# Unrolling the first layer of a two-layer encoder step, with score jobs in pairs and the weights' low parts on VectorE

## What is computed

```
for i in range(2):                                     # layer 0: diff, layer 1: fox
    h = rmsnorm(x, norm_mix[i])
    x = x + mixer(h) @ w_o                             # 1024x1024
    h = rmsnorm(x, norm_ffn[i])
    gate, up = split(h @ w_in, 2)                      # 1024 x 2*2816
    x = x + (silu(gate) * up) @ w_out                  # 2816x1024
y = rmsnorm(x, norm_final)

def diff_mixer(h):                                     # per group: two heads share V
    q, k, v = split(h @ w_qkv); q, k = rope(q), rope(k)
    p1, p2 = softmax(q1 @ k1.T / 8 + mask), softmax(q2 @ k2.T / 8 + mask)
    o = (p1 - lam * p2) @ v
    return rmsnorm(o, subln) * 0.8
```

## Time and profile before

| | us |
|---|---|
| median of 3 runs (lowest to highest) | 1607.44 (1604.28 to 1611.6) |
| the profiled execution | 1607.57 |
| its span, first to last instruction | 1605.4 |
| TensorE busy in the span | 1563.1 |
| VectorE / GpSimd / ScalarE busy | 619.9 / 581.5 / 560.9 |

### The profile page before, as it was taken

One profiled execution on the slowest core, in us unless ns is written; L12 is line 12 of the kernel. 1 busy time (PEld: TensorE's weight loads), 2 busy tenths in 40 slices (PEclk: granted clock), 3 DMA queues, 4 the chain that ended last, 5 costly groups with the idle time before them and its releaser, 6 DMA issues.

```text
span 1605.4 us, 29879 instructions
## 1 busy us (share of the span) xinstructions
PE 1563.1 (97%) x11071; PEld 1476.8 (92%) x11071; DVE 619.9 (39%) x1091; ACT 560.9 (35%) x995; POOL 581.5 (36%) x276
## 2 busy tenths in 40 slices
PE   6999999999999999999999999999999999999996
PEld 5888888999999999999978888888999999999996
DVE  6667776451111111121366666665521111111212
ACT  4455545442222222222334444444332222232221
POOL 3333233334544444333322222221344455444331
PEclk9999999999999999999999999999999999999998
DMA  5322223122222222222211211111122222222222
GB/s 188 98 85 83 95 85 107 41 79 79 78 82 88 78 78 85 76 82 85 94 62 61 62 60 60 60 57 48 67 79 85 85 78 78 91 78 74 83 83 82
DMA packets 44628, 128.49 MB, mean 80 GB/s; under 512 B 5648, under 2 KB 10256, under 8 KB 44576
## 3 DMA queue, kind: packets, MB, share of 16 engines
q1 hardware_dynamic: 44576, 127.79, 23.6%
HBM read 111.21 MB, written 11.83 MB: 77 GB/s over the span
## 4 chain that ended last, share of the span: by engine, by line
PE 91%; DVE 5%; issue 2%; ACT 1%; DMA 1%; SPq 0%; DVEq 0%; ACTq 0%
PE ps L486 73%; PE sps L534 3%; PE ops L597 3%; PE tps L554 2%; PE sps L540 2%; PE sps L535 2%; PE sps L536 2%; PE sps L542 1%; PE ops L587 1%; DVE acc L1164 1%; DVE aug_l L1303 1%; DVE xT L1173 0%; PE tps L568 0%; DVE ptl L1269 0%; PE ops L604 0%
## 5 line engine op out<-in xcount | busy, mean ns | idle before, releaser
L1069 POOL TENSOR_TENSOR w_lo<-w_raw,w_hi 128x1024 fp32r<-128x1024 f32 (+1 forms) x199 | 469.4, 2359 | 922.2 <-ACT w_hi L787 922.2
L486 PE MATMUL ps<-xh,w_hi 128*128 128x288 f32 x2176 | 489.5, 307 | 18.5 <-DVE xl L1418 11.5
L486 PE MATMUL ps<-xl,w_hi 128*128 128x288 f32 x2176 | 468.7, 297 | 0.0
L486 PE MATMUL ps<-xh,w_lo 128*128 128x288 f32 x2176 | 468.3, 297 | 0.0
L486 PEld LDWEIGHTS ps<-xh,w_hi 128*128 128x128 f32 x2176 | 350.2, 191 | 20.4 <-issue 19.9
L787 ACT ACTIVATE w_hi<-w_raw 128x1024 fp32r<-128x1024 f32 (+1 forms) x200 | 208.3, 1042 | 451.7 <-PE ps L486 449.5
L486 PEld LDWEIGHTS ps<-xh,w_lo 128*128 128x128 f32 x2176 | 352.9, 190 | 0.0
L486 PEld LDWEIGHTS ps<-xl,w_hi 128*128 128x128 f32 x2176 | 352.8, 190 | 0.0
L866 ACT ACTIVATE pr<-sps,nmax 128x384 f32<-128x384 f32 (+3 forms) x160 | 85.9, 537 | 205.4 <-DVE nmax L1233 188.4
L486 PE MATMUL ps<-hh,w_hi 128*128 128x288 f32 x704 | 150.9, 295 | 0.0
L486 PE MATMUL ps<-hl,w_hi 128*128 128x288 f32 x704 | 150.8, 295 | 0.0
(11 more groups left out here) (154 smaller groups left out, 1768.6 us busy)
## 6 DMA issues: line engine op xcount, KB each, us to landing
w_raw<-w_units SPq DMA_DIRECT2D x184, 512.0 KB, 3.2
w_raw<-w_units SPq DMA_DIRECT2D x16, 384.0 KB, 2.8
qsw<-qsin SPq DMA_DIRECT2D x64, 72.0 KB, 2.0
xT<-x_in SPq DMA_DIRECT2D x8, 288.0 KB, 5.6
dk_out<-kf SPq DMA_DIRECT2D x8, 288.0 KB, 2.1
dv_out<-vf SPq DMA_DIRECT2D x8, 288.0 KB, 4.1
fk_out<-kf SPq DMA_DIRECT2D x8, 288.0 KB, 4.1
fv_out<-vf SPq DMA_DIRECT2D x8, 288.0 KB, 4.0
```

Source lines behind the costliest of these rows:

```text
L486: mm = nc.tensor.matmul(out[:, half, :], w[:, k, :], rhs[:, kt, half * HALF:(half + 1) * HALF], start=start and w is w_hi[slot] and rhs is ...
L1069: nc.gpsimd.tensor_tensor(w_lo[slot][:, 0:kts, :], w_raw[slot][:, 0:kts, :], w_hi[slot][:, 0:kts, :].bitcast(F32), ALU.subtract).then_inc( ...
```

## The change

The first layer is written out whole, without loops, by a count t of slots from its start. Each engine goes through all t and has, for every step of a group's attention, a slot of its own in tables (`D_SCORE`, `D_MAX`, `D_EXP`, ...; s is the slot counted from the start of the next group). Beside that:

- `score_pair` takes the place of two score jobs.
- the first head's scaling goes from VectorE to ScalarE (`weigh_first`), and each head has a reciprocal of its own.
- VectorE makes w_lo of units 2 to 24 (`weight_lo`); GpSimd keeps the others.
- in both layers V is split straight out of PSUM, in three pieces, vl by VectorE (`v_lo`); the cached V has a buffer v_raw.
- the head norm's squares are made by ScalarE; GpSimd has nothing left in the first layer's groups.
- in both layers the output projection has 14 runs in another order, and the preparation of the tiles is spread over its steps by tables (`WO_RES_AT`, `WO_HI_AT`, `WO_LO_AT`, `WO_SQ_AT`, `WO_SUM_AT`), with two buffers for the squares. The norm sum moves from slice 6 of the FFN's first unit to slice 2 of its second, and in the second layer's first unit from slice 6 to its end.
- SP issues the first layer's transfers by the same count t.

```diff
+WO_STEPS = ([(j, 4 + j, k) for j in (0, 1, 2) for k in range(6)]
+            + [(j, j - 2, k) for j in (3, 4, 5) for k in range(7)]
+            + [(6, 0, k) for k in range(KT)]
+            + [(6 + t, t, 7) for t in (1, 2, 3)]
+            + [(6 + t, t, k) for t in (4, 5, 6) for k in (6, 7)]
+            + [(13, 7, k) for k in range(KT)])
...
+D_SCORE, D_MAX, D_EXP, D_DEN, D_SCALE, D_MIX = (3, 5, 11, 14, 19), (2, 5, 10, 13, 20), ...
+D_TURN, D_TAKE_P, D_P_LO = (8, 12, 17, 19, 27), (8, 12, 16, 21, 26), (7, 12, 15, 19, 26)
+D_W_LO = 3
+D_SPLIT = 1
...
+            def score_pair(a, par, p):
+
+                i = JOBS[DIFF][2 * p][0]
+                if some(a * 10 + 2 * p):
+                    pe.wait_ge(exp_done, val(a * 10 + 2 * p))
...
+                for x, y, first in ((qh, kh, True), (qh, kl, False), (ql, kh, False)):
+                    for h in range(2):
+                        b = slice(64 * h, 64 * h + 64)
+                        nc.tensor.matmul(sps[:, h, 0:width(i)], x[par][b, q], y[par][b, k], start=first, stop=False)
+                d = 0 if i == 4 else i
+                for h in range(2):
+                    nc.tensor.matmul(sps[:, h, P * d:P * d + P], ident16, mask[DIFF], start=False, stop=True
+                                     ).then_inc(s_done, 1)
...
-                        if tt == 0:
-                            pe.wait_ge(vr_done, val((a + (G * L + 1)) * 2))
+                            pe.wait_ge(vl_done, val((a + G) * 3 + 1))
...
-                    if k == 6 and norm > 0:
-                        norm_sum(norm)
...
                 if L == FOX:
-
+                    norm_sum(2)
                     pe.wait_ge(f_hi_done, 1)
                     pe.wait_ge(f_lo_done, 1)
                     pe.wait_ge(r_ready, 3)
...
+                    if k == NORM_AT:
+                        norm_sum(2 * L + 1)
...
+            def weigh_first(a, par, p):
+
+                w, tau, sa = width(JOBS[DIFF][2 * p][0]), a.c * 5 + p, (10 * par + 2 * p) % 4
+                act.wait_ge(rden_done, 2 * tau + 1)
+                nc.scalar.activation(pr[:, sa, 0:w], pr[:, sa, 0:w], ACT.Copy, scale=rden[:, sa:sa + 1]
+                                     ).then_inc(pa_done, 1)
...
+            def weight_lo(u):
+
+                slot = u % 2
+                dve.wait_ge(w_hi_done, u + 1)
+                dve.wait_ge(w_used, u - 1)
+                tt(w_lo[slot][:], w_raw[slot][:], w_hi[slot][:].bitcast(F32), ALU.subtract).then_inc(w_lo_done, 1)
...
+            def v_lo(L, a):
+
+                gi = a + G * L
+                for b, hi, src in ((0, vh[:, 0:4, :], tps[:]), (1, vh[:, 4, :], ops[:, 0:P]), (2, vh[:, 5:7, :], v_raw[:])):
+                    dve.wait_ge(vh_done, val(gi * 3 + (b + 1)))
+                    dst = (vl[:, 0:4, :], vl[:, 4, :], vl[:, 5:7, :])[b]
+                    tt(dst, src, hi.bitcast(F32), ALU.subtract).then_inc(vl_done, 1)
...
+                    if t % KT == D_W_LO and KT <= t < SLOTS * G:
+                        weight_lo(t // KT + 1)
+                    if t >= SLOTS * G:
+                        wo_residuals(DIFF, t - SLOTS * G)
+                    diff_attention(t)
```

More of the change, by code:

```diff
@@ L220, in encoder @@
         hf = place("hf", [P, T])
-        sqt = place("sqt", [P, T], offset=ARENA - 4 * T)
+        sqt = [place(f"sqt{s}", [P, T], offset=ARENA - 4 * T * (s + 1)) for s in range(2)]
         sq_all = place("sq_all", [P, KT, T], offset=o_at)
@@ L619, in attention @@
-                for tt in range(len(T_AT[L])):
-                    if T_AT[L][tt] == slot:
+                    if S_AT[FOX][jj] == slot:
+                        score(a, par, jj)
+                for tt in range(len(T_AT[FOX])):
+                    if T_AT[FOX][tt] == slot:
                         if tt == 0:
-                            pe.wait_ge(vr_done, val((a + (G * L + 1)) * 2))
-                            if L == DIFF and not first:
-                                pe.wait_ge(oln_done, val(a))
-                        transpose_p(L, a, par, tt)
@@ L636, in group, with project @@
+            def project(L, g, slot):
+                u, n = g * 3 + U_LAYER * L, g * 3 + N_LAYER * L
+                part, k = slot // KT, slot % KT
+                if k == 0:
+                    open_unit(u + part, n + part)
+                mm = slice_(u + part, n + part, k, xh, xl, k, k == 0, k == KT - 1)
+                if k == KT - 1:
+                    mm.then_inc(w_used, 1)
+            def group(g, par, first=False):
                 lag = 1 if first else 0
@@ L728, in _ @@
+                mm = slice_(Num(u + q // KT), Num(n + j), q % KT, oh, ol, k, q == WO_OPEN[j], q == WO_END[j])
+                if q % KT == KT - 1:
+                    mm.then_inc(w_used, 1)
+                elif q == WO_END[j]:
+                    mm.then_inc(wo_done, 1)
             for L in (DIFF, FOX):
                 first_group(L)
-                group(L, Num(1), 1, first=True)
-                with pe.Fori(0, 3) as it:
-                    for par in range(2):
-                        group(L, Num(2 + par, 2, it), par)
@@ L924, in attention, with wo_prep, fox_attention @@
+            def wo_prep(L, q):
+                for k in range(KT):
+                    if WO_HI_AT[k] == q:
+                        act.wait_ge(ps_read, N_LAYER * L + N_WO + 6 + k + 1)
+                        prep_hi(2 * L + 1, Num(k))
+                    if WO_SQ_AT[k] == q:
+                        prep_square(2 * L + 1, Num(k))
+            def fox_attention(a, par, slot, first=False):
                 if slot == 0 and not first:
-                    take_o(L, a - 1, L)
+                    take_o(FOX, a - 1, 1)
@@ L945, in attention, with group @@
+                for h in range(2):
+                    if PVS_AT[FOX][h] == slot:
+                        take_o_sample(FOX, a, h)
+                    if PVP_AT[FOX][h] == slot:
+                        take_o(FOX, a, h)
+                    if PVS_AT[FOX][h] + 1 == slot:
                         o_hi_sample(a, h)
-            def group(L, g, par, first=False, alone=False):
-                u = g * 3 + U_LAYER * L
+            def group(g, par, first=False, alone=False):
+                u = g * 3 + U_LAYER
@@ L949, in group @@
                 for slot in range(SLOTS):
                     if not alone:
-                        attention(L, g - 1, 1 - par, slot, first)
-                    if alone and L == FOX and slot == 0:
+                        fox_attention(g - 1, 1 - par, slot, first)
+                    if alone and slot == 0:
                         act.wait_ge(f_loaded, 16)
@@ L1320, in attention @@
[L1320 to L1326 removed]
+                    if S_AT[FOX][jj] + 1 == slot:
+                        weigh(a, par, jj)
+                for t in range(len(T_AT[FOX])):
+                    if T_AT[FOX][t] == slot:
+                        p_lo(FOX, a, t)
@@ L1327, in attention, with group @@
+                for h in range(2):
+                    if PVS_AT[FOX][h] == slot:
+                        o_sum(FOX, a, h)
+                    if PVS_AT[FOX][h] + 2 == slot:
                         o_lo_sample(a, h)
-                    if PVP_AT[L][h] == slot:
+                    if PVP_AT[FOX][h] == slot:
                         o_lo(a, h)
-            def group(L, g, par, first=False, alone=False):
+            def group(g, par, first=False, alone=False):
                 for slot in range(SLOTS):
```

702 lines of the change are left out of this document (390 added, 312 removed).

## The result

The changed kernel takes 1569.91 us (median of 4 runs, 1567.91 to 1570.72), the kernel before 1608.38 beside it: ratio 0.976, 95% interval 0.9735 to 0.9785. The profiled execution took 1567.91 us, 39.7 us less than that of before, and its span is 1566.1 us, 39.3 us less; the forecast was 41.6 us less.

What follows compares the result with a forecast made beforehand. TensorE's own instruction stream, busy 97% of the span, was taken as the bound. From 1607.57 us, -33.5 - 1.0 - 3.3 - 7.4 + 1.2 + 2.4 = -41.6 gave 1566 us, range 1557 to 1575 (chance 0.62).

Steps and rivals of the forecast that it cites:

- Score pairs: First layer's groups: two heads' score matmuls run at once, saving 4.19 us a group, 33.5 us in all.
- transposes: First layer's groups: two of five transpose runs stand directly beside a pair, saving 1.0 us in all.
- VectorE's order: First layer's groups, slots 8 and 12: strict order makes TensorE wait 0.3 us a group, 2.4 us lost.
- rival "VectorE's order": First layer's groups: VectorE's order becomes the bound, two waits of 0.9 us a group, 1580 us; chance 0.14.
- Hand-over: First group to second: later first score, one low-part wait gone, no half-clock stretch, 3.3 us saved.
- End of the output projections: Both layers, into the FFN: the 2.2 us wait and the half clock go, 3.7 us each, 7.4 us saved.
- Second layer's start: Norm sum behind the first unit: the forget projection waits for its result at once, 1.2 us lost.
- V's low part on VectorE in the second layer: Second layer's groups: moved from GpSimd, ahead of one row maximum a group; no effect, ends -1 and +4 us.

Runs made afterwards that it cites:

- extra_on_vector: Changed kernel with one more VectorE instruction, an unread maximum of about 1.2 us, ahead of each low part of units 2 to 24: 1584.48 us.
- pairs_alone: Kernel before with score pairs as its one change, loops, shared slots and GpSimd's low parts kept: 1594.01 us, ratio 0.9923.
- pairs_vector_lo: Kernel before with score pairs, and the low parts of units 2 to 24 made by VectorE: 1579.78 us, ratio 0.9826.
- split_first: Changed kernel with the high part of the FFN's second unit ahead of tile 7's preparation on ScalarE, both layers: 1569.08 us.
- sums_last: Changed kernel with FFN units two and three's high parts and second layer's norm sum earlier, VectorE's sums for tiles 5 to 7 later: 1564.82 us.
- norm_back: Changed kernel with the norm sum of the second layer's start back at slice 6 of its first unit: 1567.67 us, ratio 0.9755.
- one_by_one: Changed kernel with the first head's three matmuls ahead of the second's in each pair, both masks after: 1570.25 us, ratio 0.9776.
- mask_between: Changed kernel with the first head's three matmuls and mask ahead of the second head's three and mask: 1599.63 us, ratio 0.9948.

## Why the prediction was right, point by point

**Score pairs and transposes, with VectorE's order: 33.5 + 1.0 - 2.4 = 32.1 us forecast, 8 x 4.09 = 32.7 measured.** The mechanism was right, and the runs name its parts: the heads at once 2.41 us a period (forecast 2.34), one change of shape instead of two 1.39 (forecast 1.85), all else that differs in the period 0.28 (forecast for transposes less VectorE's order: -0.2). The pair's sum was thus 0.4 us a period too high, and the two small terms as much too low; that they cancelled was luck. The about 4 ns per tile that the Trainium skill states ("TensorE: Matmul & The Clock Gate", section "Measured speedup vs the span model") held here: the two matmuls of a pair start 3 to 4 ns apart by the trace's start times.

**VectorE's order: 0.3 us a group forecast, no wait seen in the periods.** The sum of its work was 1.2 us too high (24.6 against 23.4), 0.5 of it because a low part takes 1.22 us and not 1.38. That the order was tight was right all the same: with three instructions of 1.2 us more a period TensorE waits. The rival "VectorE's order" did not happen, by a margin that extra_on_vector bounds at less than 3.6 us a period.

**What the prediction did not see** is how the parts hang together. It priced the pairs for themselves and GpSimd's relief as time that VectorE gets back. In pairs_alone the same pairs bring 13 us, since a faster TensorE arrives at a wait that the slower one never met. The sum came out right because the change brings pairs and cures together.

**Hand-over, and all else up to the first layer's last projection unit: 3.3 us forecast, 34.5 - 32.7 = 1.8 measured.** The wait for the low part of unit 2 grew from 1.36 to 1.72 us, as was said; that of unit 3 is gone; the scores still wait 0.75. What the step left out is that the whole hand-over hangs on the first norm's scale, and ScalarE came to that at 26.93 us here and at 25.01 before, 1.9 us later, behind a stretch at a lower clock. Most of this is no effect of the change: pairs_alone and pairs_vector_lo have the start of the kernel before, and there the clock fell as well and the scale came at 26.18 and 26.38; the kernels with the changed start lie at 26.17 to 27.54. Whether the last half microsecond is the change's, one profile of each can't say. Without the 1.9 us the step gives 3.7, close to the forecast.

**End of the output projections: 7.4 us forecast, 1.9 + 3.1 = 5.0 measured.** This is the term that was mis-sized. The step said that the whole wait goes and with it the half clock, and both went. But it asked only what the first FFN unit waits for, not the second, whose high part stands behind tile 7 on ScalarE. Before, that unit's low part was just as late (it ended 7.6 us behind the first FFN slice's start, then as now), but the 2.2 us wait, the half clock and the norm sum in its first unit (8.9 us for that unit, 6.6 now) had delayed TensorE enough to hide it. In the second layer a wait of 0.79 us for a transpose also went (at 1126.82 before), which no step had priced. With the waits at the second and third unit the places add up: 3.7 - 1.16 - 0.38 = 2.2 us in the first layer, 3.7 + 0.79 - 1.15 - 0.36 = 3.0 in the second. What the step and its rows overlooked is that the old wait was in good part the meeting of GpSimd and VectorE too: just ahead of the residual of tile 6 a low part takes 2.39 us (at 341.57, beside GpSimd's of 340.95), where the others take 0.81. split_first and sums_last show how the waits are chained: moving the high part alone shifts the wait to tiles 6 and 7, moving VectorE's sums as well removes most of it.

**Second layer's start: 1.2 us lost forecast, 1.1 measured**, by the mechanism named (the new wait is 1.64 us); norm_back brings it back. **V's low part on VectorE in the second layer: nothing forecast, 0.1 lost.** The 0.9 us won at the end comes from the clock: the last norm sum, which the change leaves as it is, ran at a granted clock of 0.50 in the profiled execution of before (2.29 us) and at 1.00 in that of after (1.24).

## What to carry to other kernels

Matmuls that contract over 64 rows gain by running two at once on different halves of the array if no full-height matmul stands between them (2.41 us of a period here); more than half of the gain of such a change can then hang on whether the other engines are ready for the faster stream (13 us came of some 33 in pairs_alone). When a stall is taken away, ask the same question of the next unit that was asked of the first, since the stall had been the cover for whatever is late next. Where GpSimd and VectorE work side by side, look at which VectorE instruction starts behind a GpSimd one, and let it be one for which nobody waits.

## What the runs showed of the hardware

- **The fourth matmul of a pair starts 10 ns behind the first.** In one_by_one the two heads' first matmuls start together at 157.08, though two matmuls of the first head stand between them in the program. The Trainium skill ("TensorE: Matmul & The Clock Gate", section "The mechanism") has matmuls start and end strictly in program order; here the measurement says otherwise, at least for the starts. So it does not hold in this case that TensorE starts every matmul in its order. A matmul over all rows is not passed (mask_between, 173.14 behind 172.99). Whether the array's queue or something ahead of it lets it pass, the profile doesn't show; it doesn't show the order in which the stream reached the chip either, though 10 ns here against 3 to 4 in turns speaks against the same stream.
- **VectorE waits out GpSimd's whole instruction, or doesn't notice it.** In pairs_alone a split of K, which reads two tiles in SBUF, starts 0.38 us behind a low part on GpSimd and takes 2.96 us; the low part of transposed probabilities just ahead of it, which reads one operand from PSUM, takes the same 0.42 us as without GpSimd:

```profile
160.21 2.39 POOL L1090 TENSOR_TENSOR w_lo<-w_raw,w_hi 128x1024 fp32r<-128x1024 f32 x1 [8.90 <-ACT w_hi L808]
160.25 0.42 DVE L1290 TENSOR_TENSOR ptl<-tps,pth 128x256 fp32r<-128x256 f32 x1
160.59 2.96 DVE L1242 TENSOR_TENSOR kl<-kf,kh 128x896 fp32r<-128x896 f32 x1
```

  The Trainium skill ("SBUF — State Buffer", section "Who interferes with whom") states it as a lock that a VectorE instruction with two SBUF inputs and a GpSimd instruction that reads SBUF take for the whole instruction, whichever starts first. The rows agree: 2.96 us end 0.95 us behind GpSimd's end, about the 1.08 that the split takes alone. Two groups earlier the split starts first, at 95.65, and takes 1.08; there it is GpSimd's low part, at 95.73, that takes 3.25 us.
